# Attention of a two-block model: reciprocal sums by way of DRAM, outputs scaled six units later

## The reference, cut to what matters

```python
def _attend(q, k, v):
    s = jnp.einsum('bqkgd,btkd->bkgqt', q, k).astype(jnp.float32) * (HEAD_DIM ** -0.5)
    p = jax.nn.softmax(s, axis=-1).astype(v.dtype)
    return jnp.einsum('bkgqt,btkd->bqkgd', p, v)
```

```python
    o_a = (a_att * jax.nn.silu(a_z)) @ w_o_a
    o_b = (b_att * jax.nn.silu(b_z)) @ w_o_b
```

## Time and profile before

| what | value |
|---|---|
| three runs | 2626.46, 2627.93, 2628.32 us |
| median | 2627.93 us |
| span of the profiled execution | 2625.6 us (its own total is not given) |
| TensorE busy | 2575.6 us, 98% of the span |
| VectorE, ScalarE, GpSimd busy | 1327.4, 829.9, 856.6 us |
| attention of layer 0 | about 1565 to 1720 us of the span |
| attention of layer 1 | about 2248 to 2376 us |
| granted TensorE clock | 0.996 of full speed on average |

### The profile page before, as it was taken

One profiled execution on the slowest core, in us unless ns is written; L12 is line 12 of the kernel. 1 busy time (PEld: TensorE's weight loads), 2 busy tenths in 40 slices (PEclk: granted clock), 3 DMA queues, 4 the chain that ended last, 5 costly groups with the idle time before them and its releaser, 6 DMA issues.

```text
span 2625.6 us, 40326 instructions
## 1 busy us (share of the span) xinstructions
PE 2575.6 (98%) x15424; PEld 1910.1 (73%) x15424; DVE 1327.4 (51%) x2373; ACT 829.9 (32%) x1783; POOL 856.6 (33%) x716
## 2 busy tenths in 40 slices
PE   5899999999999999999999999999999999999999
PEld 2677777775788878888884567765555567778887
DVE  3455555551555567777842256533224513753324
ACT  3334444442312122222002347731111223663221
POOL 0222222220555525556543222022323043103444
PEclk9999999999999999999999999999999999999999
DMA  6211111113145434454322210001111122101222
GB/s 222 70 45 46 38 45 45 33 33 145 65 145 184 153 114 159 167 185 161 134 89 70 88 50 24 1 33 65 57 56 57 56 85 81 41 1 49 97 81 96
DMA packets 61410, 220.93 MB, mean 84 GB/s; under 512 B 6784, under 2 KB 8960, under 8 KB 60992
## 3 DMA queue, kind: packets, MB, share of 16 engines
q1 hardware_dynamic: 42576, 153.11, 17.2%
q0 software_dynamic: 14656, 56.89, 6.3%
q10 hardware_dynamic: 4016, 8.65, 0.9%
HBM read 214.90 MB, written 2.15 MB: 83 GB/s over the span
## 4 chain that ended last, share of the span: by engine, by line
PE 94%; DVE 2%; DMA 1%; ACT 1%; issue 1%; ACTq 0%; POOL 0%; DVEq 0%; SPq 0%
PE psum L456 90%; PE psum L969 3%; DMA arena<-in_conds 1%; DMA arena<-in_stream 1%; PE psum L1027 0%; ACTq L1284 0%; PE psum L689 0%; ACT arena L1423 0%; DVE arena L2047 0%; DVE arena L2019 0%; ACT arena L1393 0%; PE psum L652 0%; ACT arena L1411 0%; POOL arena L2743 0%; DVE arena L2080 0%
## 5 line engine op out<-in xcount | busy, mean ns | idle before, releaser
L456 PE MATMUL psum<-arena 128*128 128x256 f32 (+10 forms) x14544 | 2473.0, 352 | 46.2 <-DVE arena L1765 12.5
L456 PEld LDWEIGHTS psum<-arena 128*128 128x128 f32 (+4 forms) x14544 | 1815.6, 170 | 685.8 <-issue 252.8
L2789 POOL TENSOR_TENSOR arena<-arena 128x512 f32<-128x512 f32 (+1 forms) x104 | 137.6, 1323 | 772.5 <-DMA arena<-in_stream 399.5
L2034 DVE TENSOR_TENSOR arena<-psum,arena 128x256 f32<-128x256 f32 (+1 forms) x103 | 47.3, 459 | 291.2 <-PE psum L456 282.1
L2005 DVE SCALAR_TENSOR_TENSOR arena<-arena 128x1024 f32<-128x1024 f32 x128 | 170.8, 1383 | 0.0
L2040 DVE TENSOR_TENSOR arena<-psum,arena 128x256 f32<-128x256 f32 (+1 forms) x103 | 47.5, 461 | 234.1 <-PE psum L456 230.1
L2793 POOL TENSOR_TENSOR arena<-arena 128x512 f32<-128x512 f32 (+1 forms) x104 | 133.2, 1280 | 96.0 <-PE psum L456 90.5
L2800 POOL TENSOR_TENSOR arena<-arena 128x512 f32<-128x512 f32 (+1 forms) x104 | 144.3, 1388 | 36.9 <-PE psum L456 36.6
L2797 POOL TENSOR_TENSOR arena<-arena 128x512 f32<-128x512 f32 (+1 forms) x104 | 138.1, 1328 | 45.2 <-PE psum L456 38.5
L1447 ACT ACTIVATE arena<-psum 128x256 f32<-128x256 f32 (+1 forms) x103 | 42.7, 414 | 307.1 <-PE psum L456 307.1
L2743 POOL TENSOR_TENSOR arena<-arena 128x512 f32<-128x512 f32 x16 | 22.1, 1402 | 315.1 <-ACT arena L1356 315.1
(11 more groups left out here) (281 smaller groups left out, 1826.9 us busy)
## 6 DMA issues: line engine op xcount, KB each, us to landing
arena<-in_stream SPq DMA_DIRECT2D x288, 512.0 KB, 3.8
arena<-in_mods POOLq DMA_DIRECT2D x80, 512.0 KB, 5.8
arena<-gc_rows POOLq DMA_DIRECT2D x16, 384.0 KB, 4.8
arena<-in_bias POOLq DMA_DIRECT2D x16, 384.0 KB, 3.9
arena<-in_xT ACTq DMA_DIRECT2D x2, 1024.0 KB, 14.0
arena<-in_conds ACTq DMA_DIRECT2D x1, 1536.0 KB
arena<-arena POOLq DMA_DIRECT2D x4, 384.0 KB, 4.3
out<-arena SPq DMA_DIRECT2D x3, 512.0 KB, 6.1
```

Of the source, the lines that this page charges most:

```text
L456: return pe.matmul(out, lhsT, rhs, start=start, stop=stop, skip_group_check=True)
L2789: add(sums[0], a21, a22, ALU.add).then_inc(s("wsum"), 1)
```

## The change

The reciprocals of a unit go into a ring of four groups (`recs`). GpSimd's queue writes them to a DRAM array sum_rows, two numbers per partition, so that the queries of a head come to lie one behind the other: one transfer of 128 x 2 single numbers per latent unit, two per context unit (80 in all). Once a group is written, two transfers read the two heads' rows back, each broadcast over 64 partitions (48 in all), into one of two buffers (`rsums`). Values go to bank 6 or 7 by the parity of the group, and the first values of a group wait for the to_att of two groups before. to_att is multiplied by 0.5 alone; a new product in place, times_sums, follows six iterations after the group's last unit, and for the last groups of a layer in the second pair of the Z stage. spread, copy_sums and widen are gone, and so is ScalarE's wait for the last to_att ahead of the Z stage. On GpSimd the writes and reads stand in the loop over the units among the table loads and negations; the first Z pair's weight sums move to the fifth far unit, and the other three behind the last broadcast.

```diff
--- before.py
+++ after.py
@@ -124,6 +124,7 @@
         arena = ctx.enter_context(nc.sbuf_tensor("arena", [P, 53000], F32))
         psum = ctx.enter_context(nc.psum_tensor("psum", [P, 8, 512], F32))
         gc_rows = nc.dram_tensor("gc_rows", (2 * HEADS, TOK), F32).ap()
+        sum_rows = nc.dram_tensor("sum_rows", (3 * 2 * PAIRS, 2, SEQ), F32).ap()
         sems = {}
 
         def s(name):
@@ -288,7 +289,8 @@
         rsum_at = sp2.at - SEQ
         HT2 = sp2.take(4 * 4 * WIDE)
         snaps2 = sp2.take(WIDE), sp2.take(WIDE), arena[:, rsum_at:rsum_at + WIDE]
-        inv_sums = arena[:, rsum_at + SEQ + 16 * WIDE:][:, 0:4 * P].rearrange("p (a b) -> p a b", a=2)
+        recs = sp2.take(4, 2 * XC)
+        rsums = sqb[:, 1, 0:SEQ], rnorm[:, 0:SEQ]
         MG2 = arena[:, MG2_AT:MG2_AT + KT * TOK].rearrange("p (a b) -> p a b", a=KT)
         n2 = Region(MG2_AT, 53000)
         hsq, hrn, rt1 = n2.take(2, TOK), n2.take(2, TOK), rsum
@@ -366,6 +368,10 @@
         def att_before(l, p):
 
             return 2 * p if l == 0 else 4 * PAIRS + p
+
+        def sums_sent(group):
+
+            return 16 * sum(CC if n % 2 and n < 4 * PAIRS else XC for n in range(group % 2, group + 1, 2))
 
         def biased(p, q):
 
@@ -984,10 +990,13 @@
                     near = biased(p, q)
                     pe.wait_ge(s("at_ptc"), g + u + 1)
                     pe.wait_ge(s("at_ptx"), tx_before(l, u + 1))
+                    if u == 0:
+                        pe.wait_ge(s("b2_vb"), 2 * l + 2)
                     if u == len(us) - 1:
                         first_z()
-                    if b == 0 and (g + u):
-                        pe.wait_ge(s("at_att"), att_before(l, p) + q)
+                    group = att_before(l, p) + q
+                    if b == 0 and group >= 2:
+                        pe.wait_ge(s("at_att"), group - 1)
                     if near and b in (1, 2):
                         pe.wait_ge(s("at_vs"), 32 * (l + 1))
 
@@ -1010,23 +1019,10 @@
                         for c in chunks:
                             for a in range(2):
                                 at = prob_at(a, c, b2)
-                                m = mm(psum[half(a), 6, (b + b2) * P:(b + b2 + 1) * P], weight(a, c),
+                                m = mm(psum[half(a), 6 + group % 2, (b + b2) * P:(b + b2 + 1) * P], weight(a, c),
                                        PT[:, u % 2, at:at + P], c == chunks[0], c == CH - 1)
                                 if c == CH - 1 and (not q or b2):
                                     m.then_inc(s("at_pv"), 1)
-
-                def spread(u):
-
-                    p, q, b = us[u]
-                    pe.wait_ge(s("at_wide"), g + u + 1)
-                    if u == 0:
-                        pe.wait_ge(s("b2_vb"), 2 * l + 2)
-                    if b == 0 and (g + u):
-                        pe.wait_ge(s("at_rc"), att_before(l, p) + q)
-                    for b2 in range(CC if q else 1):
-                        m = pe.transpose(psum[:, 7, (b + b2) * P:(b + b2 + 1) * P],
-                                         inv_sums[:, u % 2, b2 * P:(b2 + 1) * P], ident)
-                    m.then_inc(s("at_rs"), 1)
 
                 for u in range(len(us) + 2):
                     if u < len(us):
@@ -1036,7 +1032,6 @@
                     if 1 <= u <= len(us):
                         transposes(u - 1)
                     if u >= 2:
-                        spread(u - 2)
                         values(u - 2)
 
             for l in range(2):
@@ -1576,34 +1571,13 @@
                                   bias=st[:, 0, o:o + 1], accum_out=st[:, 1, o:o + 1])
                         m.then_inc(s("at_P"), 1)
 
-                def copy_sums(u):
-                    p, q, b = us[u]
-                    act.wait_ge(s("at_rs"), g + u + 1)
-                    act.wait_ge(s("at_att"), att_before(l, p) + q)
-                    w = CTX if q else SEQ
-                    f(rsum[:, 0:w], psum[:, 7, 0:w], ACT.Copy).then_inc(s("at_rc"), 1)
-
-                def widen(u):
-                    o, n = stat(u, 0), CC if us[u][1] else 1
-                    act.wait_ge(s("at_ri"), g + u + 1)
-                    if g + u >= 2:
-                        act.wait_ge(s("at_rs"), g + u - 1)
-                    for b2 in range(n):
-                        v = st[:, 2, o + b2:o + b2 + n + 1:n, None].to_broadcast([P, 2, HD])
-                        m = f(inv_sums[:, u % 2, b2 * P:(b2 + 1) * P].rearrange("p (a d) -> p a d", a=2), v, ACT.Copy)
-                    m.then_inc(s("at_wide"), 1)
-
-                for u in range(len(us) + 3):
-                    if 1 <= u <= len(us):
+                for u in range(len(us) + 1):
+                    if u:
                         evict(u - 1)
-                    if 2 <= u < len(us) + 2 and last(us[u - 2]):
-                        copy_sums(u - 2)
                     if u < len(us):
                         exps(u)
                     if u == 0:
                         context_values()
-                    if 1 <= u <= len(us):
-                        widen(u - 1)
 
             for l in range(2):
                 wide = l == 0
@@ -1657,7 +1631,6 @@
                         .then_inc(s("b2_vb"), 1)
 
                 attention(l, context_values)
-                act.wait_ge(s("at_att"), att_before(l, 2 * PAIRS))
                 w = half_of(l)
                 banks = (0, 2, 3), (1, 2, 3)
                 ended = None
@@ -2430,17 +2403,28 @@
                     dve.tensor_copy(PT[:, u % 2, SEQ:2 * SEQ], score_banks(l, u)[:, SEQ:2 * SEQ]).then_inc(s("at_ptc"), 1)
 
                 def recip(u):
-                    o, n = stat(u, 0), 4 if us[u][1] else 2
+                    p, q, b = us[u]
+                    o, n = stat(u, 0), 2 * CC if q else 2
+                    group = att_before(l, p) + q
                     dve.wait_ge(s("at_P"), 2 * (g + u) + 2)
-                    dve.reciprocal(st[:, 2, o:o + n], st[:, 1, o:o + n]).then_inc(s("at_ri"), 1)
+                    dve.reciprocal(recs[:, group % 4, 2 * b:2 * b + n], st[:, 1, o:o + n]).then_inc(s("at_ri"), 1)
 
                 def to_att(u):
                     p, q, b = us[u]
-                    dve.wait_ge(s("at_rc"), att_before(l, p) + q + 1)
+                    group = att_before(l, p) + q
                     dve.wait_ge(s("at_pv"), 2 * (g + u + 1))
                     w, at = (CTX, SEQ) if q else (SEQ, 0)
-                    stt(ATT[:, p, at:at + w], psum[:, 6, 0:w], 0.5, rsum[:, 0:w], ALU.mult, ALU.mult)\
+                    ts(ATT[:, p, at:at + w], psum[:, 6 + group % 2, 0:w], 0.5, None, ALU.mult)\
                         .then_inc(s("at_att"), 1)
+
+                def times_sums(u):
+                    p, q, b = us[u]
+                    group = att_before(l, p) + q
+                    w, at = (CTX, SEQ) if q else (SEQ, 0)
+                    dve.wait_ge(s("at_att"), group + 1)
+                    dve.wait_ge(s(f"R{group % 2}"), 32 * (HEADS // 2 + group // 2 + 1))
+                    v = ATT[:, p, at:at + w]
+                    tt(v, v, rsums[group % 2][:, 0:w], ALU.mult).then_inc(s("at_norm"), 1)
 
                 for u in range(len(us) + 3):
                     if u >= 3 and last(us[u - 3]):
@@ -2452,6 +2436,15 @@
                     if 1 <= u <= len(us):
                         evict(u - 1)
                         recip(u - 1)
+                    if u >= 6 and last(us[u - 6]):
+                        times_sums(u - 6)
+
+                def rest():
+
+                    for u in range(len(us) - 3, len(us)):
+                        if last(us[u]):
+                            times_sums(u)
+                return rest
 
             for l in range(2):
                 wide = l == 0
@@ -2527,7 +2520,7 @@
                 scale(11)
                 turn(3)
                 scale(12)
-                attention(l, lambda: turn(4))
+                rest_of_sums = attention(l, lambda: turn(4))
 
                 w = half_of(l)
                 banks = (0, 2, 3), (1, 2, 3)
@@ -2547,6 +2540,9 @@
                     join_first(n, y, snaps2, KA[:, 0, 0:w], w)
                     join_second(n, z, snaps2, KA[:, 0, w:2 * w], w)
                     join_fourth(n, x, snaps2, KA[:, 1, w:2 * w], w)
+                    if j == 1:
+                        rest_of_sums()
+                        dve.wait_ge(s("at_norm"), att_before(l, 2 * PAIRS))
                     dve.wait_ge(s("zt"), 8 * l + 2 * j + 1)
                     stt(KA[:, 2, 0:2 * w], KA[:, 2, 0:2 * w], 1.0, KA[:, 0, 0:2 * w], ALU.add, ALU.mult)\
                         .then_inc(s("zs"), 1)
@@ -2881,6 +2877,34 @@
                     qk_sums(n)
                 negate_tables(0)
                 negate_tables(1)
+                def write_sums(u):
+
+                    p, q, b = us[u]
+                    n = att_before(l, p) + q
+                    pool.wait_ge(s("at_ri"), g + u + 1)
+                    for b2 in range(CC if q else 1):
```

(38 more changed lines are left out.)

## The result

The changed kernel takes 2664.96 us (median of four runs, 2660.39 to 2668.97) where the kernel before takes 2627.19 on the same chip: ratio 1.0145, 95% interval 1.0131 to 1.0158. Forecast were 2621.2, in a range from 2618.5 to 2628.5, so the time moved the other way. It lies beyond every rival too: B, the dearest, had 2649.

The account below looks back on a forecast made before the run. TensorE's work was taken to bound attention. Removed transposes -8.2, VectorE's tight places +0.4, late negations +0.7, broadcast jitter +0.4 made -6.7 us: 2627.9 to 2621.2 us, range 2618.5 to 2628.5.

Parts of the forecast that it names:

- B: GpSimd's queue, near units: slow write issues make GpSimd the bound; +21 us, 2649 us; chance 0.11.
- the 0.7 us for the late negations: Layer 1, near units: GpSimd negates bias tables late behind writes, costing TensorE 0.1 + 0.6 = 0.7 us.
- part (b): Layer 0, near units: a context group's broadcast behind the negation just fits; 0.2 us for jitter in two pairs, 0.4 us.
- (a): GpSimd's bias-table negation behind writes: late by 0.74 and about 1.3 us in layer 1, free in layer 0; 0.7 us.
- rival A: GpSimd's element-wise writes cost 1.1 us each to issue and land late; +2.6 us, 2623.8 us; chance 0.17.
- C: Near units: transposes were free, the loop through VectorE and ScalarE sets the period; 2624.5 us; chance 0.10.
- The price of a transpose in the near units: TensorE, near units: each removed row-sum transpose saves 0.11 us, taking an iteration from 3.23 to 3.12 us.
- times_sums at 0.69: VectorE's new product: 0.69 us per 512 columns, about 14 us for 24 groups, beside TensorE.
- VectorE's room in layer 1: Near units, layer 1: product plus to_att run 0.56 us late against 0.66 slack; 0.1 us in four places, 0.4 us.

Follow-up runs that it names:

- the last version: Version with reciprocals turned on VectorE and tables loaded ahead of writes, changed so layer 1's near products come eight units later, not six: 2619.17 us, ratio 0.9967 to before.

## Why the prediction was wrong

**The step that failed** is the sentence "The write lands 2.0 us later like gc_rows, or as late as 5.9 like the slowest table load." It was 8 to 11 us in the changed kernel. And the remark in the same part, that the weights' transfers share engines "which are busy for 0.11 and 0.01 of these stages", took the writes themselves for no load: 80 transfers of 1 KB. In the records of single packets those of a table load take 0.23 us in the median, before and now, and before 1.7 at most; now about every eighth takes over 1.5 us, the longest 9.6. In the sum the 0.7 us for the late negations supposed that the tables had landed (3.9 us); with 12.3 to 16.8 it became 21.9 us of VectorE's waits, 21.5 of them in layer 1. The other 17.4 are not the 0.4 us of part (b): the context groups' broadcasts behind a negation never made VectorE wait. They are above all the latent groups' broadcasts (10.0 and 6.0 us for the first two pairs), which the prediction had put at nothing, since VectorE asks "four periods (12 us or more) after its issue, against 2.0 + 1.1 + 4.8 = 8". With the write's 11.45 and the broadcast's 13.43 it was 25 in place of 8. In the near units the kernel after takes 21.9 us more than the last version in layer 0 and 23.7 in layer 1. TensorE's own waits there make 35.2 of it; the rest fits its longer pieces at the lower clock behind them.

**Where I chose wrongly.** The rule of the Trainium skill on a last dimension that isn't contiguous (DMA: Bandwidth & Descriptors, Rules for kernel authors) was before me, and I let it bear on the issue alone. The issue came out small: 0.73 us, between my 0.6 and 1.1. The nearest row for the landing, gc_rows, has 16 rows of 3 KB; it has the direction of the write and nothing of its form. A bound for the unknown form was missing, and with it the rival in which the landing fails. Rival B named the right side and the wrong place: its condition, issues of 2.3 us, was never near, and the negations came late all the same. (Its 5.4 us of lateness in layer 1 don't follow from (a) either, where a write of 3 us adds 2.4 to the 0.74 and 1.3.) Of rival A the issue cost was not met; its "land late" was the true half, but priced at 7.3 us for the broadcast and nothing for the tables. C fell: near iterations are 3.12 where nothing stalls.

**What held.**
- The price of a transpose in the near units: TensorE alone in the chain of the last version, 3.12 us an iteration (3.23 before):

```profile
1576.83 2.10 PE psum L462 x24
1578.93 1.02 PE psum L975 x8
1579.96 2.10 PE psum L462 x24
```

- In the far units of layer 0 it was too high. A pair takes 22.47 us there and took 22.87: 0.40, not 6 x 0.11 = 0.66. Of its five intervals one stayed at 4.47 and one fell by 0.07. What sets these two was not tried. In the last version attention gains 2.27 and 1.42 us in the near units and 1.47 and 1.48 in the far ones, 6.6 in all, where the transposes alone were to give 8.2.
- times_sums at 0.69: 0.67 beside nothing, 3.33 beside a negation. VectorE's room in layer 1 came out too: in the run without writes the reduction behind the product and to_att comes 0.3 us late (an interval of 3.41) and the next one makes it up (2.84), where 0.56 late was forecast to just fit. GpSimd on the other side of the same operands was not counted at all.
- Nothing is late behind attention: the span's growth is attention's, within 0.2 us.

## What to carry to other kernels

Price a small transfer by three numbers: its issue, its landing, and how long it holds up what is behind it on the same DMA engines; here its 1 KB and a low DMA share told nothing of the last two. Where no row has a form of transfer (here single numbers side by side in DRAM), the landing has no upper bound from other rows, and the rival in which it fails belongs in the range. And an instruction that is moved beside GpSimd's pass over SBUF can be several times its usual length: look what runs on that engine in the new place.

## What was not expected of the hardware

- 256 pieces of 4 bytes side by side in DRAM land in 8 to 11 us, those of the same size 64 or 512 bytes apart in 1.5 to 2.0, 16 bytes apart in 3.2, 128 pieces of 8 bytes in 6.2, 32 of 128 bytes in 1.6. That neighbours within 64 bytes are finished one after another is what the series suggests; the mechanism was not seen itself. The records of the writes' own packets (64 bytes each, 38 to 39 ns in the median) are the same at 4, 16, 64 and 512 bytes and don't show it.
- A transfer of 384 KB behind them takes up to 17.0 us (in the kernel before with the writes), and up to 15.8 from another engine's queue.
- A VectorE product of two SBUF operands took 3.33 us (alone 0.67) beside a GpSimd pass over SBUF.
- Around waits of TensorE of 2 to 10 us its granted clock was 0.63 to 0.77 in the mean of 5 to 10 us, and 24 matmuls behind them took up to 3.75 us in place of 2.10.
